# Gate vectors by one rounded product, bias and rounding on VectorE; queries split before they are turned; one weight pair loaded earlier

## The chip, the cores and the metric

The kernel runs on one core of a Trainium2 chip. The metric is device time in microseconds, from start to end of one launch: the median of three runs before the change is 1631.0 us (1630.05 to 1631.31).

## What is computed

One step of a two-layer network with width 1024 on 128 context tokens and 512 latent tokens (five token tiles of 128). Everything is float32. Each layer first makes six modulation vectors per group from a conditioning vector: shift, scale and gate of the mixer (c = 0, 1, 2) and of the MLP (c = 3, 4, 5).

```python
m = jax.nn.silu(cvec) @ w_mod + b_mod            # 1024 x 6144, per layer
hp = modulate(rmsnorm(xp, norm_mix_pre[layer]), mod_p[0], mod_p[1])
...
xp = xp + mod_p[2] * rmsnorm(yp, norm_mix_post[layer])      # gate c = 2
...
xp = xp + mod_p[5] * rmsnorm(sq_relu_mlp(hp, w_ffn_in[layer], w_ffn_out[layer]), norm_ffn_post[layer])
```

Layer 0's mixer is a gMLP beside an RG-LRU, layer 1's is attention with 16 query heads on 4 key heads of 64, window 128, a sink and 2-D rotary positions. Latent tokens also see cached context keys.

## The kernel before

A function `schedule()` writes one list of steps, and every engine walks that list in its order, waiting on semaphores. So the order of the list is the order of work on each engine. It also lists the weight loads; SP issues them in order into two slots of RAW (1 MB each), the next load waiting until its slot has been read.

**Products.** Float32 operands are split into a rounded part (float32r) and a remainder. Each product is three float32r matmuls (lines 1149 to 1151: high by high, low by high, high by low). For weights, ACT casts a block of RAW into the ring WH (line 630) and POOL subtracts to make WL (line 854); the ring has six blocks. Each step may carry a list "split" of blocks, which ACT and POOL handle behind the step's own work.

**Modulation.** A step `mod` multiplies the two columns of CL (conditioning vectors, padded to 32) with half a vector's weights: 16 plain float32 matmuls of 512 columns, in four groups of 32 PSUM rows. For a gate (c = 2 or 5) a seventeenth product of one row adds the bias from BMR into the open accumulation. VectorE copies the bank to PART. The next `mod`, or a `flush()`, first issues `modfin` for the former one. For a gate that is two plain float32 products with the selector SEL (one for context, one for latent tokens) that add the four row groups and spread them over 128 partitions; VectorE multiplies each into the gains GG (line 942). For other vectors it is four transposes (line 1210). Each layer has four gate halves, eight in all.

**MLP start.** `ffn()` issues the first weight pair's product for token tiles 0 and 1 (A, part 0), turns token tiles 3 and 4 (T, "cut"), runs the gate step (c = 5, half 0), then part 1 of the pair, then the second pair. The G2 steps are products with the second weights, one per token tile.

**Attention.** 20 units, of four heads by one token tile. Steps per unit i: S(i) scores; Q(i+1) turns the next queries; PV(i-2) transposes probabilities (line 1379) and multiplies with values (line 1387); sums; softmax(i) on VectorE (line 1114, mask and maximum) and ACT. Q turned each head's 128x64 block by a plain product with the identity (line 1340), twice, into both halves of the PSUM rows. ACT rounds the bank into QS (line 799), and VectorE subtracts the lower half from the bank (line 887, `query_remainder`), at the head of softmax.

Of the kernel before, what the change touches and what calls it, by code (L numbers as in the profile page):

```python
# [17 lines left out]
P = 128  # L18
# [18 lines left out]
def schedule():  # L37
# [23 lines left out]
    pend = []  # L61
# [8 lines left out]
    def mod(layer, c, half):  # L70
# [4 lines left out]
        pend.append((layer, c, half, cb[0]))  # L75
        cb[0] += 1
# [46 lines left out]
    def ffn(layer, fillers):  # L123
# [8 lines left out]
        ld = tiles(0, 0)  # L132
        T_(ph, TT - 2)
# [3 lines left out]
        tiles(2)  # L137
        for c in range(FC):
# [166 lines left out]
def hybrid_step(nc, A):  # L305
# [5 lines left out]
    with ctx:  # L311
# [26 lines left out]
        BMR = sb("BMR", [1, 512])  # L338
        IDN = sb("IDN", [P, P])
        SEL = sb("SEL", [P, 2, P])  # L340
# [25 lines left out]
        GGF = GG[:, :, :].rearrange("p v n -> p (v n)")  # L366
        RG = [GGF[:, i * TOK:(i + 1) * TOK] for i in range(6)]
# [10 lines left out]
        KTOK = GGF[:, 1024:2048].rearrange("p (s n) -> p s n", s=4)  # L378
        Z = GGF.rearrange("p (u h n) -> p u h n", u=2, h=4)

# [6 lines left out]
        PT = [RAW[:, PT_LOAD % RAWN, 512 * i:512 * i + 512] for i in range(4)]  # L387

# [22 lines left out]
        bmr_in = sem("bmr_in")  # L411
# [17 lines left out]
        k_out, k_hi, q_hi = sem("k_out"), sem("k_hi"), sem("q_hi")  # L429
# [170 lines left out]
        def _(act):  # L600
# [19 lines left out]
            act.dma_start(SEL[:, :, :], A["sel"]).then_inc(const_in[6], 16)  # L620
# [12 lines left out]
            for s in STEPS:  # L633
                k = s["kind"]
                if k == "mod":
                    if s["c"] in (2, 5):
                        if ngate:
                            upto(act, m_ready, GATE_M[ngate - 1])
                        ngate += 1
                        c0 = s["c"] * D + 512 * s["half"]  # L640
                        act.dma_start(BMR[:, :], A["b_mod"][s["layer"]:s["layer"] + 1, c0:c0 + 512]).then_inc(bmr_in, 16)

                        half, kind = s["half"], 0 if s["c"] == 2 else 2
                        if s["layer"] == 1:
                            for i in (18, 19):
                                upto(act, m_ready, PV_M[i])
                        elif kind:
                            act.wait_ge(x_new, TT)
                        else:
# [795 lines left out]
```

## Time and profile before

| | |
|---|---|
| median of three runs | 1631.0 us |
| the profiled execution's own time | 1628.96 us |
| its span | 1627.2 us |
| TensorE busy | 1506.1 us |
| VectorE / ACT / POOL busy | 656.2 / 554.5 / 518.1 us |
| mean granted TensorE clock | 0.968 of full speed |

The profile is one execution. The span runs from the first instruction to the last. TensorE's clock has two levels, 2.4 GHz (written 1.00) and 1.2 GHz (0.50). Rows of the timeline give start and duration in microseconds; matmuls are pipelined, so the distance between starts is their cost, and the written duration includes latency.

### The profile page before, as it was taken

What the parts mean: (1) busy time and instruction counts of PE and PEld (TensorE: products, weight loads), DVE (VectorE), ACT (ScalarE), POOL (GpSimd) and SP (SyncE); (2) the same over time, 40 slices, a digit from 0 to 9 for tenths busy, and PEclk for the clock granted to TensorE, in tenths of its full rate; (3) what the DMA queues carried; (4) which work ended last, traced back from release to release, by engine and by line L of the source; (5) the groups of instructions that cost most, each with busy time, mean ns of one, the idle gap of its engine ahead of it and who ended that gap; (6) DMA issues with size and microseconds to landing.
All of it is one profiled execution on the core that took longest, in us unless ns stands there. A gap on an engine that the chain in (4) does not pass through costs nothing.

```text
span 1627.2 us, 20069 instructions
## 1 busy us (share of the span) xinstructions
PE 1506.1 (93%) x8338; PEld 1242.4 (76%) x8338; DVE 656.2 (40%) x1124; ACT 554.5 (34%) x927; POOL 518.1 (32%) x224
## 2 busy tenths in 40 slices
PE   4799869899999999999889789989899999999997
PEld 1786646697898898998677656657689899989985
DVE  3665662733322322222644466623542232223225
ACT  3456732631221221232531266614532223222211
POOL 0521233141242243243234134413324234323330
PEclk9899979999999999999999899999899999999999
DMA  9322425144344342222022000033242122213201
GB/s 336 98 78 104 145 70 174 37 158 143 130 141 144 130 152 93 92 78 78 27 83 78 27 1 2 1 104 130 82 145 84 59 97 79 78 52 104 78 26 65
DMA packets 90498, 153.87 MB, mean 95 GB/s; under 512 B 6356, under 2 KB 44704, under 8 KB 90408
## 3 DMA queue, kind: packets, MB, share of 16 engines
q1 hardware_dynamic: 81712, 143.14, 26.7%
q10 hardware_dynamic: 8696, 9.45, 2.1%
q8 instruction: 66, 1.08, 0.3%
q14 instruction: 24, 0.20, 0.0%
HBM read 149.69 MB, written 2.89 MB: 94 GB/s over the span
## 4 chain that ended last, share of the span: by engine, by line
PE 71%; DVE 8%; ACT 5%; issue 2%; DMA 1%; POOL 1%; ACTq 0%; DVEq 0%; SPq 0%
PE PS L1149 20%; PE PS L1150 20%; PE PS L1151 20%; PE PS L1189 3%; PE PS L1387 2%; PE PS L1379 1%; DVE X L968 1%; DVE ACC L967 1%; PE PS L1357 1%; PE PS L1340 1%; PE PS L1358 1%; POOL WL L854 1%; ACT XCB L671 1%; DVE HL L988 1%; DVE HF L982 1%
## 5 line engine op out<-in xcount | busy, mean ns | idle before, releaser
L854 POOL TENSOR_TENSOR WL<-RAW,WH 128x1024 fp32r<-128x1024 f32 x172 | 422.0, 2484 | 769.2 <-ACT WH L630 769.2
L1149 PE MATMUL PS<-HH,WH 128*128 128x384 f32 (+1 forms) x1152 | 359.6, 312 | 10.4 <-DVE HL L988 5.3
L1151 PE MATMUL PS<-HH,WL 128*128 128x384 f32 (+1 forms) x1152 | 358.2, 311 | 0.0
L1150 PE MATMUL PS<-HL,WH 128*128 128x384 f32 (+1 forms) x1152 | 358.2, 311 | 0.0
L630 ACT CAST WH<-RAW 128x1024 fp32r<-128x1024 f32 x172 | 170.3, 1047 | 500.5 <-PE PS L1151 294.4
L1149 PE MATMUL PS<-WH,AH 128*128 128x512 f32 x640 | 253.3, 396 | 11.8 <-DVE AL L1003 6.5
L1150 PE MATMUL PS<-WL,AH 128*128 128x512 f32 x640 | 251.3, 393 | 0.0
L1151 PE MATMUL PS<-WH,AL 128*128 128x512 f32 x640 | 251.1, 392 | 0.0
L1149 PEld LDWEIGHTS PS<-HH,WH 128*128 128x128 f32 x1152 | 221.3, 192 | 16.1 <-issue 9.8
L1150 PEld LDWEIGHTS PS<-HL,WH 128*128 128x128 f32 x1152 | 221.5, 192 | 0.5
L1151 PEld LDWEIGHTS PS<-HH,WL 128*128 128x128 f32 x1152 | 220.9, 192 | 0.0
L1070 DVE TENSOR_TENSOR ACC<-ACC,PS 128x512 f32<-128x512 f32 x140 | 95.6, 687 | 233.3 <-PE PS L1151 233.3
L1001 DVE TENSOR_TENSOR XCB<-XCB 128x640 f32<-128x640 f32 x64 | 65.7, 1027 | 288.7 <-ACT XCB L718 288.5
L1149 PEld LDWEIGHTS PS<-WH,AH 128*128 128x128 f32 x640 | 121.1, 189 | 47.2 <-issue 8.6
L1149 PE MATMUL PS<-WH,HH 128*128 128x512 f32 x360 | 147.7, 410 | 8.7 <-POOL WL L854 5.4
L1150 PE MATMUL PS<-WL,HH 128*128 128x512 f32 x360 | 142.7, 396 | 0.0
L1151 PE MATMUL PS<-WH,HL 128*128 128x512 f32 x360 | 142.6, 396 | 0.0
L1151 PEld LDWEIGHTS PS<-WH,AL 128*128 128x128 f32 x640 | 121.3, 189 | 25.8
L1150 PEld LDWEIGHTS PS<-WL,AH 128*128 128x128 f32 x640 | 121.2, 189 | 24.7 <-issue 0.2
L718 ACT ACTIVATE XCB<-PS 128x640 f32<-128x640 f32 x64 | 45.1, 705 | 199.7 <-PE PS L1151 199.7
L1003 DVE TENSOR_TENSOR AL<-XCB,AH 128x640 fp32r<-128x640 f32 x64 | 76.7, 1198 | 50.7 <-ACT AH L724 50.7
L1149 PEld LDWEIGHTS PS<-WH,HH 128*128 128x128 f32 x360 | 69.1, 192 | 35.4 <-issue 10.9
(160 smaller groups left out, 1552.3 us busy)
## 6 DMA issues: line engine op xcount, KB each, us to landing
RAW<-in_w_mod SPq DMA_DIRECT2D x42, 1024.0 KB, 5.1
RAW<-in_w_ffn_in SPq DMA_DIRECT2D x32, 1024.0 KB, 5.7
RAW<-in_w_ffn_out SPq DMA_DIRECT2D x32, 1024.0 KB, 4.9
RAW<-in_w_in_even SPq DMA_DIRECT2D x8, 1024.0 KB, 6.8
RAW<-in_w_qkv SPq DMA_DIRECT2D x6, 1024.0 KB, 5.4
EARLY_H<-in_w_mod SPq DMA_DIRECT2D x4, 1024.0 KB, 21.2
RAW<-in_w_out_even SPq DMA_DIRECT2D x4, 1024.0 KB, 5.5
RAW<-in_w_out_odd SPq DMA_DIRECT2D x4, 1024.0 KB, 5.2
```

What stands on the lines that cost most here:

```text
L630: nc.scalar.copy(ring_view(WH, ld, j), w_view(ld, b)).then_inc(w_hi, 1)
L671: link(nc.scalar.activation(JUNK, ACC[:, t, :], ACT.Square, accum_out=STAT[:, t, 0:1]))
L718: nc.scalar.activation(XC[0], a_bank(a), ACT.Relu).then_inc(a_free[a % 2], 1)
L854: nc.gpsimd.tensor_tensor(ring_view(WL, ld, j), w_view(ld, b), ring_view(WH, ld, j).bitcast(f32), ALU.subtract).then_inc(w_lo, 1)
L1001: V_.tensor_tensor(XC[1], XC[0], XC[0], ALU.mult).then_inc(sq_ready, 1)
L1003: V_.tensor_tensor(AL[:, slot, :], XC[1], AH[:, slot, :].bitcast(f32), ALU.subtract).then_inc(a_lo, 1)
L1070: V_.tensor_tensor(acc, acc, bank, ALU.add).then_inc(b_free[b % 2], 1)
L1149: MM(out, wh, xh, start=first, stop=False)
L1150: MM(out, wh, xl, start=False, stop=False)
L1151: return MM(out, wl, xh, start=False, stop=last)
L1189: ins = MM(PS[32 * kt:32 * kt + 32, 6 + u % 2, :], CL[:, 4 * kh + kt, :], rv[:, kt, :], start=(kh == 0), stop=(kh == 1 and not gate))
L1387: ins = MM(PS[64 * par:64 * par + 64, 6 + u % 2, 0:256], vv(keys[kt])[:, HD * g:HD * g + HD], pt[:, par, :, :], start=(kt == 0), stop=(kt ...
```

## The change

Four edits:

1. CL gets its two columns a second time, so rows 2 and 3 of each group of 32 repeat rows 0 and 1. The bias product is gone. A new step `modsplit` on VectorE adds the bias to PART, rounds it into PARTR, and turns rows 2 and 3 into remainders with a per-partition factor (PICK). The selector SELR has ones for both, so `modfin` of a gate is one float32r product per token group. TensorE waits on `part_split` for it.
2. `modsplit` is put behind the next B group or the next G2 step.
3. Queries are split by VectorE on token rows (`query_split`: a cast and a subtraction, both from and to SBUF) before four transposes per unit; the ACT copy is the only later step, and `query_remainder` is gone.
4. In `ffn()` the load of the second pair stands ahead of the gate's two loads.

```diff
+    def modsplit():
+        if unsplit:
+            c, half = unsplit.pop()
+            step("modsplit", c=c, half=half)
     def flush():
+        modsplit()
         if pend:
...
     def bgroup(what, nb, t, j, ph=None):
         step("B", uses_b=1, frees=4 if t == TT - 1 else 0, what=what, nb=nb, t=t, j=j, ph=ph)
+        modsplit()
...
         ld = tiles(0, 0)
+        ld2 = load("acols", src=("w1", layer), col=2 * P)
         T_(ph, TT - 2)
         T_(ph, TT - 1)
         mod(*fill.pop(0))
         tiles(0, 1, ld)
-        tiles(2)
+        tiles(2, None, ld2)
...
                 step("G2", uses_b=2, frees=4 if t == TT - 1 else 0, layer=layer, c=c, t=t, j=j, ph=ph + 1)
+                modsplit()
                 if t in (0, 2) and fill and not last:
                     mod(*fill.pop(0))
...
-                    nc.scalar.copy(QS[:, i % 2, :], m_bank(u)).then_inc(q_hi, 1)
+                    nc.scalar.copy(QS[:, i % 2, :], m_bank(u)).then_inc(m_free[u % 2], 1)
...
+            def query_split(i):
+
+                g, t = i % NKV, i // NKV
+                if i > 1:
+                    upto(dve, m_ready, Q_M[i - 2])
+                q = ACC[:, t, 256 * g:256 * g + 256].rearrange("p (h d) -> p h d", h=4)
+                hi, lo = (Q2[i % 2].rearrange("p (h w d) -> p h w d", h=4, w=2)[:, :, w, :] for w in (0, 1))
+                V_.tensor_copy(hi.bitcast(f32r), q).then_inc(q_hi, 1)
                 dve.wait_ge(q_hi, i + 1)
-                V_.tensor_tensor(QS[64:128, i % 2, :], m_bank(u)[64:128, :], QS[64:128, i % 2, :].bitcast(f32),
-                                 ALU.subtract).then_inc(m_free[u % 2], 1)
+                V_.tensor_tensor(lo, q, hi, ALU.subtract).then_inc(q_split, 1)
...
+                elif k == "modsplit":
+                    ngate += 1
+                    upto(dve, m_free, part_u)
+                    dve.wait_ge(bmr_in, 16 * ngate)
+                    V_.tensor_tensor(PART[0:4, :], PART[0:4, :], bias_row(s["c"], s["half"]), ALU.add).then_inc(bias_read, 1)
+                    dve.wait_ge(bias_read, ngate)
+                    if ngate == 1:
+                        dve.wait_ge(sel_made, 1)
+                    link(V_.tensor_copy(PARTR[:, :], PART[:, :]))
+                    V_.scalar_tensor_tensor(PARTR[:, :], PARTR[:, :].bitcast(f32), PICK[:, 2:3], PART[:, :], ALU.mult, ALU.add)\
+                        .then_inc(part_split, 1)
...
-                                MM(PS[0:32, 6 + u % 2, :], SEL[0:1, 0, 0:32], BMR[:, :], start=False, stop=True)
...
                     if s["c"] in (2, 5):
+                        ngate += 1
+                        pe.wait_ge(part_split, ngate)
                         for v in (0, 1):
                             u = s["m"] + v
                             m_acquire(u)
-                            MM(m_bank(u), SEL[:, v, :], PART[:, :], start=True, stop=True).then_inc(m_ready[u % 2], 1)
+                            MM(m_bank(u), SELR[:, v, :], PARTR[:, :], start=True, stop=True).then_inc(m_ready[u % 2], 1)
...
-                    for h in range(4):
-                        c = HD * (4 * g + h)
-                        for half in (0, 64):
-                            ins = MM(m_bank(u)[half:half + 64, P * h:P * h + P], ACC[:, t, c:c + HD], IDN[:, :], start=True, stop=True)
+                    pe.wait_ge(q_split, s["n"] + 1)
+                    for h in range(4):
+                        ins = TR(m_bank(u)[:, P * h:P * h + P], Q2[s["n"] % 2][:, P * h:P * h + P], IDN[:, :])
```

**VectorE at the first gate half of layer 0's MLP.** COPY ACC is the first token tile of the first G2 steps, GG the gains. Before:

```order
L1001 TENSOR_TENSOR XCB<-XCB 128x640 [waits a_lo,a_hi,a_free1]
L1003 TENSOR_TENSOR AL<-XCB,AH 128x640 [waits a_hi]
L1072 COPY ACC<-PS 128x512 [waits b_ready0]
L1072 COPY ACC<-PS 128x512 [waits b_ready1]
L942 TENSOR_TENSOR GG<-PS,GG 128x512 [waits gg_in0,m_ready0]
L942 TENSOR_TENSOR GG<-PS,GG 128x512 [waits gg_in0,m_ready1]
L932 COPY PART<-PS 128x512 [waits m_ready1,m_ready0]
```

The same place in the changed kernel:

```order
L1047 TENSOR_TENSOR XCB<-XCB 128x640 [waits a_lo,a_hi,a_free1]
L1049 TENSOR_TENSOR AL<-XCB,AH 128x640 [waits a_hi]
L1120 COPY ACC<-PS 128x512 [waits b_ready0]
L1120 COPY ACC<-PS 128x512 [waits b_ready1]
L972 TENSOR_TENSOR PART<-PART,GG 4x512 [waits bmr_in,m_free1]
L976 CAST PARTR<-PART 128x512 [waits bias_read]
L977 SCALAR_TENSOR_TENSOR PARTR<-PARTR,PICK,PART 128x512 [waits dve_done]
L988 TENSOR_TENSOR GG<-PS,GG 128x512 [waits gg_in0,m_ready0]
L988 TENSOR_TENSOR GG<-PS,GG 128x512 [waits gg_in0,m_ready1]
L966 COPY PART<-PS 128x512 [waits m_ready1,m_ready0]
```

Three operations now stand between the copies of the G2 step and the product that TensorE issues right behind that step. The `modfin` follows at once in the list here, and likewise in layer 1.

**VectorE in a late attention unit.** AST holds the softmax's small values, COPY RAW moves turned probabilities. Before:

```order
L1120 SCALAR_TENSOR_TENSOR AST<-AST,SINK 128x4 [waits z_ready]
L1121 TENSOR_SCALAR AST<-AST 128x4 [waits dve_done]
L1122 TENSOR_TENSOR AST<-SINK,AST 128x4 [waits dve_done]
L895 TENSOR_TENSOR HL<-PS,HH 128x2x128 [waits mix_hi]
L504 COPY RAW<-PS 128x512 [waits m_ready1,pt_mm0]
L504 COPY RAW<-PS 128x512 [waits m_ready1,pt_mm1]
L1130 TENSOR_TENSOR AST<-AST 128x4 [waits es_ready,e_ready]
L1131 RECIPROCAL AST<-AST 128x4 [waits dve_done]
L887 TENSOR_TENSOR QS<-PS,QS 64x512 [waits q_hi]
L1114 ISA GG,AST<-PS,XCB 128x512 [waits s_done,pt_mm1]
```

And in the changed kernel:

```order
L1166 SCALAR_TENSOR_TENSOR AST<-AST,SINK 128x4 [waits z_ready]
L1167 TENSOR_SCALAR AST<-AST 128x4 [waits dve_done]
L1168 TENSOR_TENSOR AST<-SINK,AST 128x4 [waits dve_done]
L920 TENSOR_TENSOR HL<-PS,HH 128x2x128 [waits mix_hi]
L911 CAST PART<-ACC 128x4x64 [waits m_ready0]
L913 TENSOR_TENSOR PART<-ACC,PART 128x4x64 [waits q_hi]
L523 COPY RAW<-PS 128x512 [waits m_ready1,pt_mm0]
L523 COPY RAW<-PS 128x512 [waits m_ready1,pt_mm1]
L1176 TENSOR_TENSOR AST<-AST 128x4 [waits es_ready,e_ready]
L1177 RECIPROCAL AST<-AST 128x4 [waits dve_done]
L1160 ISA GG,AST<-PS,XCB 128x512 [waits s_done,pt_mm1]
```

The one subtraction ahead of the mask step has become two operations that stand earlier, behind the former unit's softmax.

**POOL around layer 0's MLP start.** WL rows are weight remainders, HL rows the remainders of turned token tiles. Before:

```order
L835 TENSOR_TENSOR GG<-GG 128x640 [waits a_free1,h_ready]
L837 TENSOR_TENSOR MX<-MX,GG 128x640 [waits h_sum]
L854 TENSOR_TENSOR WL<-RAW,WH 128x1024 [waits w_hi] x10
L849 TENSOR_TENSOR HL<-HF,HH 128x4x128 [waits h_hi] x5
L854 TENSOR_TENSOR WL<-RAW,WH 128x1024 [waits w_hi] x64
```

And POOL at this place in the changed kernel:

```order
L855 TENSOR_TENSOR GG<-GG 128x640 [waits a_free1,h_ready]
L857 TENSOR_TENSOR MX<-MX,GG 128x640 [waits h_sum]
L874 TENSOR_TENSOR WL<-RAW,WH 128x1024 [waits w_hi] x10
L869 TENSOR_TENSOR HL<-HF,HH 128x4x128 [waits h_hi] x2
L874 TENSOR_TENSOR WL<-RAW,WH 128x1024 [waits w_hi] x2
L869 TENSOR_TENSOR HL<-HF,HH 128x4x128 [waits h_hi] x3
L874 TENSOR_TENSOR WL<-RAW,WH 128x1024 [waits w_hi] x62
```

Two weight blocks (the second pair) moved between the token tiles' remainders 1 and 2; ACT's two casts for them moved with them, ahead of the norm of token tile 4.

## Rows read from the trace of the kernel before

**Rows 1.** The page: busy times, and the chain that ended last.

```profile
PE 1506.1 (93%) x8338; PEld 1242.4 (76%) x8338; DVE 656.2 (40%) x1124; ACT 554.5 (34%) x927; POOL 518.1 (32%) x224
...
PE 71%; DVE 8%; ACT 5%; issue 2%; DMA 1%; POOL 1%; ACTq 0%; DVEq 0%; SPq 0%
```

**Rows 2.** Timeline of TensorE (start, duration): gate steps in layer 0's MLP.

```profile
371.20 1.88 PE L1205 MATMUL PS<-PART,SEL 128*128 128x512 f32 x4
373.01 1.90 PE L1189 MATMUL PS<-RAW,CL 128*32 128x512 f32 x10
...
376.80 0.50 PE L1149 MATMUL PS<-WH,AH 128*128 128x512 f32 x1
```

**Rows 3.** The same timeline: the following modulation step, which is no gate.

```profile
389.63 1.92 PE L1189 MATMUL PS<-RAW,CL 128*32 128x512 f32 x16
391.48 0.50 PE L1149 MATMUL PS<-WH,AH 128*128 128x512 f32 x1
```

**Rows 4.** The same timeline: the kernel's first step, and the gate step at MLP start.

```profile
9.18 3.64 PE L1189 MATMUL PS<-RAW,CL 128*32 128x512 f32 x16 [9.18 <-DVE CL L873]
...
321.10 2.59 PE L1189 MATMUL PS<-RAW,CL 128*32 128x512 f32 x10 [1.98 <-DVE HF L982]
...
327.48 0.69 PE L1149 MATMUL PS<-HH,WH 128*128 128x384 f32 x1
```

**Rows 5.** Timeline of VectorE beside Rows 2.

```profile
371.40 0.69 DVE L1072 COPY ACC<-PS 128x512 f32<-128x512 f32 x1 [1.70 <-PE PS L1151]
372.25 0.69 DVE L942 TENSOR_TENSOR GG<-PS,GG 128x512 f32<-128x512 f32 x1 [0.17 <-PE PS L1205]
```

**Rows 6.** The page's costliest groups (busy, mean ns | idle); durations of L988 (min/median/max).

```profile
L854 POOL TENSOR_TENSOR WL<-RAW,WH 128x1024 fp32r<-128x1024 f32 x172 | 422.0, 2484 | 769.2 <-ACT WH L630 769.2
...
L988 DVE TENSOR_TENSOR HL<-HF,HH x20: 691/1224/2886, 40.6 to 1161.6; 128x512 fp32r<-128x512 f32 x20
```

**Rows 7.** Windows: busy time of PE, PEld, DVE, ACT, POOL; granted clock; DMA.

```profile
769.70:775.90 6.20, 5.82 (x14) 4.56 (x15) 0.62 (x2) 1.36 (x2) 4.70 (x2) 0.50 0.01 4
1144.50:1147.20 2.70, 0.07 (x2) 0.04 (x1) 2.68 (x3) 2.05 (x5) 1.64 (x1) 1.00 0.00 0
1148.00:1151.20 3.20, 3.20 (x19) 3.20 (x18) 3.13 (x7) 3.17 (x9) 0.00 (x0) 0.53 0.00 0
```

**Rows 8.** Timeline around layer 0's MLP start.

```profile
308.10 0.57 ACT L759 COPY ACC<-PS 128x512 f32<-128x512 f32 x1
...
317.98 1.15 PE L1221 MATMUL PS<-IDN,ACC 128*128 128x128 f32 x8 [1.19 <-DVE HF L982]
...
323.42 1.26 POOL L849 TENSOR_TENSOR HL<-HF,HH 128x512 fp32r<-128x512 f32 x1 [2.64 <-ACT HH L702]
...
329.61 2.00 ACT L630 CAST WH<-RAW 128x1024 fp32r<-128x1024 f32 x2 [6.28 <-DMA RAW<-in_w_ffn_in]
```

**Rows 9.** Timeline of late attention units.

```profile
981.15 1.09 PE L1340 MATMUL PS<-IDN,ACC 128*64 128x128 f32 x16
...
989.34 1.09 PE L1340 MATMUL PS<-IDN,ACC 128*64 128x128 f32 x16
...
994.25 0.69 DVE L1114 CUSTOM_DVE_ANT_0 GG<-PS,XCB 128x512 f32<-128x512 f32 x1 [0.79 <-PE PS L1379]
...
997.30 0.42 DVE L895 TENSOR_TENSOR HL<-PS,HH 128x256 fp32r<-128x256 f32 x1
...
998.02 1.09 PE L1340 MATMUL PS<-IDN,ACC 128*64 128x128 f32 x16
...
999.04 1.09 PE L1379 MATMUL PS<-IDN,GG 128*128 128x128 f32 x8
```

**Rows 10.** Timeline of the first attention units.

```profile
915.44 2.55 DVE L1052 TENSOR_TENSOR ACC<-ACC,GG 128x512 f32<-128x512 f32 x1
...
918.02 0.70 DVE L887 TENSOR_TENSOR QS<-PS,QS 64x512 fp32r<-64x512 f32 x1
...
926.18 1.98 PE L1340 MATMUL PS<-IDN,ACC 128*64 128x128 f32 x16
```

More of the change, by code:

```diff
@@ L75, in mod @@
         pend.append((layer, c, half, cb[0]))
+        if c in (2, 5):
+            unsplit.append((c, half))
         cb[0] += 1
@@ L337, in hybrid_step @@
         PART = sb("PART", [P, 512])
-        BMR = sb("BMR", [1, 512])
+        Q2B = alias("Q2B", [P, 512])
+        PARTR = sb("PARTR", [P, 512], f32r)
         IDN = sb("IDN", [P, P])
-        SEL = sb("SEL", [P, 2, P])
+        SELR = sb("SELR", [P, 2, P], f32r)
+        PICK = sb("PICK", [P, 3])
         CC = sb("CC", [P, 2, KD])
@@ L387, in hybrid_step, with bias_row @@
         PT = [RAW[:, PT_LOAD % RAWN, 512 * i:512 * i + 512] for i in range(4)]
+        def bias_row(c, half):
+            return GG[0:4, 3 if c == 2 else 0, 512 * half:512 * half + 512]
         def vv(t):
@@ L636, in _ @@
                     if s["c"] in (2, 5):
+                        half, kind = s["half"], 0 if s["c"] == 2 else 2
+                        if kind:
+                            act.wait_ge(x_new, TT if s["layer"] == 0 else 3 * TT)
+                        elif s["layer"] == 1:
+                            for i in (18, 19):
+                                upto(act, m_ready, PV_M[i])
+                        else:
+                            act.wait_ge(rg_done, 4)
+                            act.wait_ge(sel_made, 1)
                         if ngate:
-                            upto(act, m_ready, GATE_M[ngate - 1])
+                            act.wait_ge(bias_read, ngate)
                         ngate += 1
                         c0 = s["c"] * D + 512 * s["half"]
[L641 to L649, printed above, removed]
-                            act.wait_ge(rg_done, 4)
+                        act.dma_start(bias_row(s["c"], half), A["b_mod"][s["layer"]:s["layer"] + 1, c0:c0 + 512].broadcast_to([4, 512]))\
+                            .then_inc(bmr_in, 16)
                         g = A["norm_mix_post" if kind == 0 else "norm_ffn_post"][s["layer"]:s["layer"] + 1, 512 * half:512 * half + 512]
@@ L907, in _ @@
                 elif k == "lambda":
+                    dve.wait_ge(const_in[5], 16)
+                    dve.wait_ge(const_in[6], 16)
+                    low = IDN[:, :].rearrange("p (g w) -> p w g", g=4)[:, 2:4, :]
+                    link(V_.tensor_reduce(PICK[:, 0:2], low, AX.X, ALU.add))
+                    for v in (0, 1):
+                        V_.tensor_scalar(SELR[:, v, :], SELF[:, v, :], PICK[:, v:v + 1], None, ALU.add)
+                    link(V_.tensor_tensor(PICK[:, 2:3], PICK[:, 0:1], PICK[:, 1:2], ALU.add))
+                    V_.tensor_scalar(PICK[:, 2:3], PICK[:, 2:3], -1.0, None, ALU.mult).then_inc(sel_made, 1)
                     lam = PC[:, LAM:LAM + 8]
@@ L1180, in _ @@
                     if s["n"] == 0:
-                        pe.wait_ge(cl_ready, 1)
+                        pe.wait_ge(cl_ready, 2)
                     for kh in (0, 1):
```

35 lines of the change are left out of this document (14 added, 21 removed).

## The prediction

> **What bounds the kernel now.** I read the page first: TensorE is busy 93% of the span, and 71% of the chain that ended last is its work [rows 1]. So I take the kernel as a queue of matmuls. An edit is worth what it takes from TensorE's queue or adds to it as waiting; work on other engines counts where TensorE waits for it. I then read TensorE's timeline at the gate steps, VectorE's beside it, the granted clock behind long waits, and the attention units, where TensorE and VectorE release each other in turn.
>
> **The gate steps without the bias product.** In the timeline a gate step runs from 373.01 to 376.80, 3.79 us [rows 2]. A step with the same sixteen products and no bias takes 389.63 to 391.48, 1.85 us [rows 3]. The difference, 1.94 us, is more than the bias product itself, since the four row groups no longer overlap around it. Six of the eight gate halves run at the full clock: 6 x 1.94 = 11.6 us less. The other two open an MLP; they are worked out below with the moved load.
>
> **The two selector products.** For a gate they take 371.20 to 373.01, 1.81 us for two products [rows 2]. The trace has float32r products of 512 columns everywhere; one lasts 0.50 us [rows 3], half of it latency that overlaps with the next, so I take 0.25 us each, 0.5 for both. What follows decides how much of the 1.3 us counts:
>
> - Three gate halves are followed by a token tile's product, which needs neither bank: 3 x 1.3, say 3.8 us less.
> - Three are followed by the next modulation step with no wait for rounding. That step needs the first bank back from VectorE. VectorE first finishes the token tile's copy (from 0.20 us after the products' start, for 0.69) and then multiplies 0.69 [rows 5], so the bank is free at about 0.2 + 0.69 + 0.03 + 0.69 = 1.6 us where it was 1.8. That is 0.2 us less each, 0.6 in all.
> - Two, one per layer (the first half of c = 5), get the new wait.
>
> **The new wait.** There `modsplit` stands directly ahead of `modfin`: both come behind the same G2 step, so the rounding isn't hidden by a group at all. VectorE's queue after the last matmul, from 0: wait and copy until 0.89 [rows 5]; bias add over 512 columns, a subtraction of that width takes 0.69 when undisturbed [rows 6], until 1.61; the cast, which no row shows, between half of that and all of it (0.35 and 0.69; I take 0.5, since a single input should cost less), until 2.15; the multiply-add, of the same width, 0.7, until 2.9; a hand-over of 0.05 to 0.1. TensorE stands from 0.2 to 3.0. Its first product takes 0.45 with latency, VectorE's multiply 0.17 + 0.69 [rows 5], so the next modulation step starts at 4.4 instead of 1.81. That is 2.6 us later, twice: +5.2 us. With the cast's bounds it is 2.4 to 2.8 each.
>
> The clock adds to it. After TensorE had stood for some 2.6 us at 1144.5 to 1147.2, the granted clock was 0.53 from 1148.0 to 1151.2; another wait, ahead of 769.7, was followed by 6.2 us at 0.50 [rows 7]. Half speed costs half of that, 1.5 and 3.1 us. The new wait (2.8 us, then 0.8 more before the modulation step) is as long. I take 2.0 each, +4.0 us, with bounds 0 and 6.2.
>
> **The MLP start and the moved load.** The gate step there began at the low clock and, with its bias, lasted 321.10 to 327.48, 6.4 us; sixteen products without bias at the low clock take 3.64 [rows 4], 2.7 less. But ACT now casts the pair's two blocks behind the copy at 308.10, 2.00 us [rows 8], ahead of the norm of token tile 4. That tile was turned at 317.98, when a wait for VectorE ended, a few tenths after it was ready; its norm now comes 2.0 us later, and POOL, with two weight blocks of 2.5 us each [rows 6], may slow VectorE beside it. I count the turn and the gate step 1.3 to 2.2 us later. POOL's last remainder, at 323.42 + 1.26 [rows 8], moves too, to about 326 to 327, and part 1 of the pair needs it: so it starts 0.5 to 1.4 us earlier than 327.48. In layer 1 the same. Together -1.9 us. The second half of the gate's load now waits until POOL has both blocks; with the casts done near 310.7 and the blocks at 2.5 us each that is near 315. The old pair's load could start only when the first half of the step at 321.10 was read, and was there at 329.61 [rows 4, 8], so a load takes at most 7 us or so: the gate's second half is there near 321 to 322, and is read a microsecond into a step that starts at 322.4. What is no longer needed is the wait for this pair behind the step.
>
> **Queries.** On TensorE, Q took 998.02 to 999.04, 1.02 us [rows 9]; eight transposes of whole 128 columns take as long as the sixteen halves did (1.09 and 1.09), so four cost 0.6 with the hand-over: -0.4 us per unit if TensorE alone counts. But VectorE must now split before it. In a late unit: the mask step starts at 994.25, when the last transposes are done, and the remainder of a former unit ends at 997.72 [rows 9]. Then come cast and subtraction of 256 columns. L895, of that size, takes 0.42, so 0.33 to 0.42 and 0.42, with hand-overs 0.85 to 0.95: the queries are ready at 998.6, 0.6 us after TensorE wanted them. The late start eats the shorter step: 998.6 + 0.6 is 999.2 against 999.04. The subtraction taken out (L887) doesn't help, since the mask step waited for TensorE anyway. Where the unit was shorter, as 981.15 to 989.34 (8.19 us against 8.68 [rows 9]), the VectorE chain is the longer by about 0.6. Of the twelve late units, four lose 0.2, two 0.1 and six about 0.5: +4.0 us.
>
> In the first six units it is the other way. There TensorE waits for VectorE and ACT, and L887 (0.70) lies on the path; a unit at the low clock turns its queries in 1.98 us [rows 10], which halves. I take -1.9 for each of two units and -0.7 for each of four: -6.6 us. Against it, the first split waits behind VectorE's last rotary addition, which ended at 917.99, where only L887 had to follow [rows 10]; now follow two splits, four transposes and a copy, 1.4 us more undisturbed. Beside POOL an addition of that width, 0.69 us undisturbed [rows 6], took 2.55 [rows 10], and POOL's weight blocks still run then: up to 2.6. I take 2.0. Attention in sum: 4.0 - 6.6 + 2.0 = -0.6 us, bounds -5 and +4.
>
> The Trainium skill says of this contention ("GPSIMD Engine Reference", Specifications) that POOL shares its SBUF interface with VectorE instructions that have two SBUF inputs or a two-port mode. The old subtraction had one SBUF input, the new one has two. By that rule alone the first unit would be at the 2.6 end; the row of 2.55 us agrees with it.
>
> **The rest** hides: six small VectorE operations for SELR and PICK stand where VectorE waits for ACT before the convolution, the second copy of CL is 0.2 us in front of a first product whose successor waits for its load, and rounding at the six other gate halves has a whole product group of over 5 us before its reader.
>
> **Sum.** -11.6 - 3.8 - 0.6 + 5.2 + 4.0 - 1.9 - 0.6 = -9.3 us. The profiled execution took 1628.96 us by its own time, the span and 1.8 us around it; it would become 1619.7. It lies 2.0 below the median of the runs, so the median goes from 1631.0 to 1621.7 us.
>
> **Rivals.**
>
> - *The new waits keep the clock up* (the two G2 waits too short, or masked by the products between): the 4.0 us fall away, and with the early attention units at their best (-5) it is 1613. For it: 1144.5 to 1147.2 itself ran at 1.00, only what came behind was slow [rows 7]. Chance 0.20.
> - *No difference.* VectorE's splits run beside POOL in the late units also, or the low clock stays as long behind each new wait as in its longest row, and the moved load gives nothing: +3 to +4 in attention, +2.2 for the clock, +1.9: 1629 to 1630. Chance 0.10.
> - *Slower: TensorE's clock falls in attention.* Every unit loses 0.86 us of plain products and gets transposes, and TensorE waits 0.6 us before them. If the granted clock then stays at 0.50 for further units, each pays: Q took 1.98 against 1.09 [rows 9, 10], and a late unit of 8.7 us, most of it TensorE, would take some 5 us more. Two such units cancel the gain, three give 1636. Against it: late units, with twelve or sixteen transposes each, ran at the full pace already [rows 9]. Chance 0.08. The Trainium skill has a rule that speaks for it ("TensorE: Matmul & The Clock Gate", Part 4: PE-mode transpose): in its words the full clock "doesn't engage" for transposes. By that rule this rival is what happens, and the time is its 1636 or more; no row here decides it.
>
> The forecast itself, 1617 to 1626, has the remaining 0.62.
>
> **Numbers.** A measurement of this kernel tells 0.2% (3.3 us) from no change. Faster needs under 1627.7: all of 0.62 and 0.20, and a little of the second rival: 0.83. Within 0.2%: 0.10. Slower: 0.07. The range 1612 to 1629 takes in the bounds of the clock (0 to 6.2), of attention and of the cast.
>
> **What would show it.** Gate steps of 1.85 us at six places and no row of BMR. A wait of TensorE of 2.5 to 3 us for VectorE's rounding (L977) once per layer at the start of the G2 steps, then a stretch at clock 0.50. In late units, TensorE waiting 0.5 us for L913 before the transposes, with unit lengths near 8.8 us; in the first ones shorter units. Part 1 of the first weight pair 0.5 to 1.4 us earlier than the sum to that point has it. It is wrong if the two G2 waits are absent, if the gate's second load is waited for, or if the clock of attention falls.

## The result, and the profile after

The changed kernel takes 1639.2 us (median of 6 runs, 1634.7 to 1644.4) against 1630.5 (6 runs) for the kernel before: ratio 1.0055, 95% interval 1.0041 to 1.0069. It is slower, where 9.3 us less was forecast. A second set of runs gave 1638.4 against 1630.7, 1.0048 (1.0036 to 1.0061). Its profiled execution took 1634.66 us with a span of 1632.9, 5.7 us over that of before.

The page of the changed kernel, in answer to [rows 1]:

```profile
PE 1472.6 (90%) x8066; PEld 1232.1 (75%) x8066; DVE 685.6 (42%) x1174; ACT 553.8 (34%) x927; POOL 521.2 (32%) x224
...
PE 65%; DVE 13%; ACT 5%; issue 2%; DMA 1%; POOL 1%; ACTq 0%; DVEq 0%
```

TensorE is busy for 33.5 us less and its part of the chain falls from 71% to 65%; VectorE's rises from 8% to 13%. Work left TensorE, and more of the time now goes into waits for VectorE.

To find the places I matched the two timelines by a product that both kernels run 2152 times in the same order (the line of the high-by-high products, L1149 before, L1195 after), and read how much later or earlier each starts than in the trace of before. The table gives the change of that distance over each stretch. A trace is one execution; the second column of the same program shows how far two differ.

| Stretch (start in the trace of before) | Forecast | Changed kernel | The same, second trace | Best version (`three`, below) |
|---|---|---|---|---|
| Front, to 208.6 us | 0 | +9.0 | +8.8 | -0.4 |
| Layer 0, c = 2 gates, to 309.8 | -5.4 | -3.2 | -3.2 | -4.1 |
| Layer 0, MLP start, to 341.5 | -1.0 | +2.0 | +4.1 | +0.8 |
| Layer 0, c = 5 gates, to 402.5 | +2.5 | +0.1 | +1.3 | -2.5 |
| MLP, QKV and attention, to 1074.6 | -0.6 | -1.3 | -1.3 | -3.4 |
| Layer 1, c = 2 gates, to 1148.0 | -5.4 | -4.0 | -4.1 | -4.5 |
| Layer 1, MLP start, to 1176.7 | -1.0 | +0.9 | +1.4 | +0.3 |
| Layer 1, first c = 5 gates, to 1524.7 | +2.7 | +3.5 | +3.7 | +4.2 |
| Last gate half | -1.3 | -1.3 | -1.3 | -1.3 |

**The front.** Nothing was forecast there, and it is more than the whole loss: 9.0 us in a trace that is 5.7 us longer in all. First VectorE, then POOL, ACT, ACT's DMA issues and TensorE of the changed kernel (start, duration):

```profile
61.36 0.16 DVE L937 TENSOR_REDUCE PICK<-IDN 128x2 f32<-128x8 f32 x1
61.56 3.46 DVE L939 TENSOR_SCALAR SELR<-GG,PICK 128x128 fp32r<-128x128 f32 x2
64.94 2.35 DVE L940 TENSOR_TENSOR PICK<-PICK 128x1 f32<-128x1 f32 x1
67.33 0.15 DVE L941 TENSOR_SCALAR PICK<-PICK 128x1 f32<-128x1 f32 x1
67.40 2.26 DVE L945 TENSOR_SCALAR LG<-PC 128x8 f32<-128x8 f32 x1
69.69 2.32 DVE L946 TENSOR_TENSOR LG<-PC,LG 128x8 f32<-128x8 f32 x1
...
62.55 9.44 POOL L874 TENSOR_TENSOR WL<-RAW,WH 128x1024 fp32r<-128x1024 f32 x4
...
72.04 0.21 ACT L677 ACTIVATE LG<-LG 128x8 f32<-128x8 f32 x1 [5.72 <-DVE LG L946]
72.05 2.69 ACTq L683 DMA_DIRECT2D MX<-in_rg_wa  x4
74.76 2.64 ACTq L683 DMA_DIRECT2D MX<-in_rg_wi  x4
77.44 0.69 ACT L732 COPY MX<-PS 128x640 f32<-128x640 f32 x1 [5.19 <-issue]
...
78.39 0.55 PE L1195 MATMUL PS<-HH,WH 128*128 128x256 f32 x1 [5.52 <-ACT MX L732]
```

Read upwards, this is a chain. TensorE waits 5.52 us for ACT's copy of a PSUM bank; ACT has eight DMA issues to do before the copy, and ahead of those an Exp (L677) that waits 5.72 us for VectorE's L946. Ahead of L946 stand the selector operations (L937 to L941), 6.0 us long. In the trace of before, the same Exp and the same copy:

```profile
62.21 2.31 DVE L912 TENSOR_TENSOR LG<-PC,LG 128x8 f32<-128x8 f32 x1
...
65.89 0.21 ACT L657 ACTIVATE LG<-LG 128x8 f32<-128x8 f32 x1
...
69.98 0.70 ACT L712 COPY MX<-PS 128x640 f32<-128x640 f32 x1 [3.88 <-issue]
```

The stall costs more than its length, since TensorE then runs at half speed for five microseconds (window of the changed kernel: from and to, length, busy time of PE, PEld, DVE, ACT and POOL, granted clock, DMA share and GB/s):

```profile
78.40:83.40 5.00, 5.00 (x23) 5.00 (x24) 0.00 (x0) 2.22 (x3) 3.65 (x2) 0.50 0.23 62
```

**The gate steps** are as forecast on TensorE: the modulation step takes 266.87 to 268.72, 1.85 us. But at the second half of c = 2 the rounding is late even where a product group lies ahead of its reader. Changed kernel, VectorE, POOL and TensorE:

```profile
275.10 2.45 DVE L972 TENSOR_TENSOR PART<-PART,GG 4x512 f32<-4x512 f32 x1
277.59 2.52 DVE L976 CAST PARTR<-PART 128x512 fp32r<-128x512 f32 x1
280.14 0.75 DVE L977 SCALAR_TENSOR_TENSOR PARTR<-PARTR,PICK,PART 128x512 fp32r<-128x512 f32 x1
...
274.61 5.21 POOL L874 TENSOR_TENSOR WL<-RAW,WH 128x1024 fp32r<-128x1024 f32 x2 [38.05 <-ACT WH L649]
...
280.99 0.70 PE L1246 MATMUL PS<-PARTR,SELR 128*128 128x512 f32 x2 [1.10 <-issue]
281.53 0.40 PE L1195 MATMUL PS<-WH,HH 128*128 128x512 f32 x1
```

Three operations that take 0.67, 0.43 and 0.75 us undisturbed (next rows) take 5.7 here. TensorE waits 1.10 and then spends 0.54 on the products, 1.64 in all, where the old step took 1.31 (it began at 273.46 before): the 0.8 us gain is a 0.3 us loss.

At the second half of c = 5 in layer 1 the same happens, and there the rounding holds up something else, VectorE's copies of the token tile behind it (VectorE, POOL and TensorE of the changed kernel):

```profile
1227.43 2.40 DVE L972 TENSOR_TENSOR PART<-PART,GG 4x512 f32<-4x512 f32 x1
1229.87 2.51 DVE L976 CAST PARTR<-PART 128x512 fp32r<-128x512 f32 x1
...
1226.89 5.21 POOL L874 TENSOR_TENSOR WL<-RAW,WH 128x1024 fp32r<-128x1024 f32 x2 [24.25 <-ACT WH L649]
...
1233.83 0.50 PE L1195 MATMUL PS<-WH,AH 128*128 128x512 f32 x1 [1.60 <-DVE ACC L1120]
```

TensorE waits 1.60 us for a bank that VectorE hasn't copied yet; the kernel before has no wait there. So three of the eight roundings (both second halves of c = 2 and this one) meet POOL's blocks, in every trace of this document.

**The new wait** at (5,0), the first half of c = 5, VectorE and then TensorE of the changed kernel:

```profile
379.77 0.67 DVE L972 TENSOR_TENSOR PART<-PART,GG 4x512 f32<-4x512 f32 x1
380.47 0.43 DVE L976 CAST PARTR<-PART 128x512 fp32r<-128x512 f32 x1
380.93 0.75 DVE L977 SCALAR_TENSOR_TENSOR PARTR<-PARTR,PICK,PART 128x512 fp32r<-128x512 f32 x1
...
381.79 0.70 PE L1246 MATMUL PS<-PARTR,SELR 128*128 128x512 f32 x2 [2.67 <-issue]
383.04 1.92 PE L1233 MATMUL PS<-RAW,CL 128*32 128x512 f32 x16 [0.55 <-DVE GG L988]
```

**The MLP start**, ACT, VectorE, POOL, TensorE, and the load on SP's queue, in answer to [rows 4, 8]:

```profile
314.88 1.99 ACT L649 CAST WH<-RAW 128x1024 fp32r<-128x1024 f32 x2
316.77 1.06 ACT L691 ACTIVATE XCB<-ACC 128x1024 f32<-128x1024 f32 x1
...
318.48 3.35 DVE L1013 SCALAR_TENSOR_TENSOR ACC<-ACC,STAT,GG 128x1024 f32<-128x1024 f32 x1
321.86 2.19 DVE L1014 TENSOR_TENSOR X<-X,ACC 128x1024 f32<-128x1024 f32 x1
...
316.00 4.74 POOL L874 TENSOR_TENSOR WL<-RAW,WH 128x1024 fp32r<-128x1024 f32 x2 [1.88 <-ACT WH L649]
320.74 2.23 POOL L869 TENSOR_TENSOR HL<-HF,HH 128x512 fp32r<-128x512 f32 x1
...
327.97 1.94 PE L1262 MATMUL PS<-IDN,ACC 128*128 128x128 f32 x8 [4.86 <-DVE HF L1028]
330.66 1.08 PE L1233 MATMUL PS<-RAW,CL 128*32 128x512 f32 x4 [0.75 <-DVE HF L1028]
...
320.77 0.37 SPq L608 DMA_DIRECT2D RAW<-in_w_mod  x1
```

The casts push the norm of token tile 4 back by 1.8 us (2.0 forecast: L691 starts 2.4 us behind the copy at 314.41, and 0.6 behind it without casts). POOL's second block now runs beside the first of VectorE's two operations of 1024 columns, and the token tile's remainder (L869), late behind the blocks, beside the other. They took 1.28 and 1.23 us undisturbed, and take 3.35 and 2.19 here. So the wait of 1.19 us in [rows 8] is 4.86. The next one, 1.98 us in [rows 4], is 0.75. Part 1 of the pair starts at 334.39, 6.9 us later than before, where the product ahead of the turns (314.73) was 6.3 later: 0.6 us later, where 0.5 to 1.4 us earlier was forecast.

### The profile page after: what moved, and what is told of

It is laid out like the page before. It is cut to its first block, busy times and chain, and to the rows that moved or that the text cites. A ratio compares the mean times of both kernels' runs of the same rounds, so it can differ in the third digit from the quotient of the medians.

```text
span 1632.9 us, 19600 instructions
## 1 busy us (share of the span) xinstructions
PE 1472.6 (90%) x8066; PEld 1232.1 (75%) x8066; DVE 685.6 (42%) x1174; ACT 553.8 (34%) x927; POOL 521.2 (32%) x224
## 4 chain that ended last, share of the span: by engine, by line
PE 65%; DVE 13%; ACT 5%; issue 2%; DMA 1%; POOL 1%; ACTq 0%; DVEq 0%
PE PS L1195 20%; PE PS L1197 19%; PE PS L1196 19%; DVE GG L1160 2%; PE PS L1233 2%; DVE ACC L1013 2%; DVE X L1014 2%; PE PS L1415 1%; PE PS L1423 1%; DMA RAW<-in_w_ffn_in 1%; ACT XCB L691 1%; ACT WH L649 1%; POOL WL L874 1%; DVE HF L1028 1%; ACT XCB L701 1%
## 5 line engine op out<-in xcount | busy, mean ns | idle before, releaser
L1195 PE MATMUL PS<-HH,WH 128*128 128x384 f32 (+1 forms) x1152 | 361.2, 314 | 19.1 <-ACT MX L732 5.5
L1195 PE MATMUL PS<-WH,AH 128*128 128x512 f32 x640 | 253.1, 395 | 13.4 <-DVE AL L1049 6.5
L1195 PEld LDWEIGHTS PS<-HH,WH 128*128 128x128 f32 x1152 | 222.4, 193 | 24.9 <-issue 18.6
L1195 PEld LDWEIGHTS PS<-WH,AH 128*128 128x128 f32 x640 | 121.2, 189 | 49.3 <-issue 8.7
L1195 PE MATMUL PS<-WH,HH 128*128 128x512 f32 x360 | 146.9, 408 | 6.3 <-POOL WL L874 3.0
L1195 PEld LDWEIGHTS PS<-WH,HH 128*128 128x128 f32 x360 | 69.0, 192 | 32.0 <-issue 10.7
```

Source lines behind the costliest of these rows:

```text
L1195: MM(out, wh, xh, start=first, stop=False)
```

## The experiments

The kernels were timed in four sets, each beside the kernel before (medians 1630.0, 1630.7, 1629.6 and 1630.4 us). Each is the changed kernel with the edit shown. The changed kernel itself stands in the second set alone, so a difference of medians between two sets is also a difference of sets; the ratios are free of that.

| Kernel | Selector block | Rounding of (5,0) | Second pair | Queries | Median us | Ratio, 95% interval |
|---|---|---|---|---|---|---|
| changed | first | late | early load | split first | 1638.4 | 1.0048 (1.0036 to 1.0061) |
| `sel_late` | last | late | early load | split first | 1629.8 | 0.9998 (0.9989 to 1.0007) |
| `sel_wait` | in the wait | late | early load | split first | 1629.3 | 0.9993 (0.9984 to 1.0002) |
| `load_old` | first | late | as before | split first | 1638.0 | 1.0048 (1.0036 to 1.0060) |
| `split_early` | first | early | early load | split first | 1630.9 | 1.0010 (1.0000 to 1.0020) |
| `q_old` | first | late | early load | as before | 1637.7 | 1.0048 (1.0035 to 1.0061) |
| `sel_split` | last | early | early load | split first | 1623.5 | 0.9955 (0.9942 to 0.9969) |
| `mid` | last | early | early load | split first | 1623.9 | 0.9957 (0.9945 to 0.9969) |
| `three` | last | early | as before | split first | 1620.8 | 0.9938 (0.9926 to 0.9950) |
| `four` | last | early | as before | as before | 1623.2 | 0.9948 (0.9931 to 0.9964) |
| `cast_late` | last | early | early load, late casts | split first | 1636.4 | 1.0043 (1.0031 to 1.0055) |
| `cast_q` | last | early | early load, late casts | as before | 1634.7 | 1.0032 (1.0020 to 1.0043) |

### The selector block (`sel_late`, `sel_wait`)

```diff
                 elif k == "lambda":
...
-                    link(V_.tensor_reduce(PICK[:, 0:2], low, AX.X, ALU.add))
...
-                    V_.tensor_scalar(PICK[:, 2:3], PICK[:, 2:3], -1.0, None, ALU.mult).then_inc(sel_made, 1)
                     lam = PC[:, LAM:LAM + 8]
...
                     V_.tensor_scalar(NCL[:, :], acc, -0.5, None, ALU.mult).then_inc(lam_ready, 1)
...
+                    link(V_.tensor_reduce(PICK[:, 0:2], low, AX.X, ALU.add))
...
+                    V_.tensor_scalar(PICK[:, 2:3], PICK[:, 2:3], -1.0, None, ALU.mult).then_inc(sel_made, 1)
```

> The changed kernel, with the selector and PICK operations moved behind the last operation of the lambda step. Theory A: their slow run beside POOL's weight blocks holds the lambda step up by about 6 us, ACT waits for it before it copies the first bank, TensorE stands 5.5 us and then runs at the low clock; nearly all of the 9 to 10 us that are lost before 170 us come back, so about 1629 us against 1639 for the changed kernel, and no TensorE wait for the first copy. Rival: the stage is late for another reason (the first product's start, the clock's phase), and the time stays within 2 us of 1639.

Measured: 1629.8 us, 8.6 less than the changed kernel (8.2 by the ratios) and level with the kernel before: theory A. In its trace (ACT) the Exp and the copy are back in their places, and TensorE doesn't wait for the copy:

```profile
65.65 0.21 ACT L677 ACTIVATE LG<-LG 128x8 f32<-128x8 f32 x1
...
69.92 0.70 ACT L732 COPY MX<-PS 128x640 f32<-128x640 f32 x1 [4.06 <-issue]
```

The second kernel puts the block two operations later only, behind the one with `lam_e` and ahead of `dve.wait_ge(lam_e, 2)`.

> The changed kernel with the selector block two instructions later: behind the two lambda operations that ACT's Exp waits for, ahead of VectorE's own wait for that Exp. This is the place that the prediction spoke of. Theory A (only the order against those two operations counts, the block's 6 us beside POOL's weight blocks are free once ACT has its input): ACT's Exp near 66 us, its first copy of MX near 70, no wait of TensorE for it, 1629 to 1631 us as with the block at the step's end. Rival (the block delays NCL, the convolution or POOL from there also): 2 us or more above that, with TensorE waiting 2 us or more longer than before at the first products that need the convolution.

Measured: 1629.3 us, theory A again. Here the block takes 7.3 us (6.0 in the changed kernel), and costs nothing (VectorE of `sel_wait`):

```profile
63.25 2.30 DVE L937 TENSOR_TENSOR LG<-PC,LG 128x8 f32<-128x8 f32 x1
...
65.67 4.61 DVE L943 TENSOR_SCALAR SELR<-GG,PICK 128x128 fp32r<-128x128 f32 x2
70.20 2.37 DVE L944 TENSOR_TENSOR PICK<-PICK 128x1 f32<-128x1 f32 x1
```

So it is neither the operations nor their slowness alone, but their standing ahead of the two that ACT waits for.

### The rounding at (5,0) (`split_early`, `sel_split`)

```diff
         T_(ph, TT - 1)
         mod(*fill.pop(0))
+        modsplit()
         tiles(0, 1, ld)
```

> The changed kernel, with the bias and rounding of the first half of c = 5 placed right behind its gate step instead of behind the first G2 step. Theory C: the two waits of 2.7 us are due to that place alone; TensorE then waits only for VectorE's multiply, 0.9 us at most, so 2.3 us less in each layer plus what the low clock cost in layer 1 (about 1.5): 1632 to 1634. Rival: the rounding now runs beside POOL's blocks, takes over 5 us and holds up VectorE's squares: no gain, 1638 or more.

Measured: 1630.9 us, 7.5 to 8.3 under the two medians of the changed kernel, more than theory C gave. Alone it could not be told from the front's loss, so both edits were joined:

> Two edits of the changed kernel at once: the selector block behind the last lambda operation, and the rounding of (5,0) directly behind its product. Theory A (the two losses lie at different places and add up: 9.4 us at the front, 6 to 8 at the two (5,0) steps): 1622 to 1624 us, that is 6 to 8 under the kernel before, and no wait over 1 us for either. Rival (part of both is the same thing, low clock that falls at other places when a wait goes): 1626 to 1629.

Measured: 1623.5 us, 6.3 under `sel_late`: the losses add up, theory A. `sel_split` is also the first version that beats the kernel before. In each of the traces with this edit, the stretch of layer 0's c = 5 gates comes 2.4 to 2.5 us ahead of before; without it it is 0.1 to 2.8 us behind. The rounding isn't slow in its new place (0.68, 0.43 and 0.75 us at 336.0 in the trace of `split_early`), and TensorE waits 0.93 us for VectorE's multiply (1218.0), as theory C has it.

In layer 1 the same edit gives less. The first c = 5 gates there are 3.5 to 5.1 us behind before without it, and still 1.5 to 4.2 with it. Most of what is left is the wait behind the second half: 0.3 to 1.9 us in the traces without the edit, 1.8 to 2.1 in all seven with it, and there each time a stretch at clock 0.50 follows. Wait and clock together cost 3.7 to 4.0 us with the edit and 0.6 to 2.2 without. No experiment took this rounding away from POOL's blocks, so what it would give is open.

The spread in layer 0 fits the clock. The changed kernel's (5,0) wait was 2.67 us in one trace and 2.66 in the other, and what followed was not the same (windows of the first and of the second trace, at the products behind the modulation step):

```profile
384.90:388.10 3.20, 3.20 (x18) 2.62 (x15) 0.80 (x2) 0.00 (x0) 0.00 (x0) 1.00 0.83 280
```

```profile
384.50:388.00 3.50, 3.14 (x17) 0.60 (x16) 1.16 (x2) 0.00 (x0) 0.00 (x0) 0.59 0.65 126
```

### The second pair's load (`load_old`, `three`, `mid`, `cast_late`)

`load_old` puts the load back behind the gate's two loads (`tiles(2)` without `ld2`).

> The changed kernel, with the second weight pair's load back behind the gate's loads. Theory B: the pair's casts and POOL blocks ahead of token tile 4's norm cost 3.7 us at each MLP start (4.9 us waits of TensorE for the turned tile, each followed by the low clock) and more in layer 1; taking them back gives 6 to 8 us, about 1632. Rival: the shorter gate step uncovers the old load, TensorE waits 2 to 3 us for the pair's remainder at each start, and half or more of the gain is gone: 1636 or above.

Measured: 1638.0 us, ratio 1.0048, equal to the changed kernel and in the rival's range. The wait of 4.9 us is gone, and one of 3.9 us (ACT's activation of the pair's first product, behind casts that waited for the DMA) has come at 344.54. With the other two faults mended:

> The two edits of sel_split, and the second pair's load behind the gate's again, as in the kernel before. Theory B (the moved load costs, since the two casts delay the norm of token tile 4 and VectorE's work beside POOL: 5 us of waiting at either MLP start, of which the old order gets 1 to 2 us each back after its own wait for the pair): 2 to 4 us less than sel_split. Rival 1 (what undoing it alone gave, 1.3 us, is all): 0 to 1.5 less. Rival 2 (the moved load gives something once the rest is undisturbed, as forecast): 1 to 2 more.

Measured: 1620.8 us, 2.7 under `sel_split`, where theory B has it. But the intervals of the two ratios overlap; taken together they leave some 3 us either way, so rival 1 isn't excluded. Over all traces but the two with late casts, the stretch of layer 0's MLP start costs 2.9 us against before with the early load (mean of 8 traces) and 3.0 with the old one (mean of 3): the wait only changes its name. In layer 1 it is +1.6 against -1.0; only there does the old order win. `three` at that product in layer 0 (TensorE):

```profile
333.94 0.35 PE L1194 MATMUL PS<-HH,WH 128*128 128x256 f32 x1 [3.00 <-ACT XCB L738]
```

> The two edits of sel_split, and the second pair's load between the last two transposes of the MLP start and the gate's loads: ahead of the gate loads still, but its casts behind the norm of token tile 5. Theory B: the wait of 4.9 us before token tile 4 goes, the wait for the pair's first block of the old order (3.9 us) does not come or is under 2 us, since the load is still early: 3 to 6 us less than sel_split and below three. Rival: the casts then keep ACT from the copies behind token tile 5 and the wait only moves: within 1.5 us of sel_split.

Measured: 1623.9 us (0.9957), but nothing on the theory: loads are numbered by their order among loads alone, no load lies between the two places, and the instructions came out as in `sel_split`. It is a second measurement of that kernel, 0.5 us from the first.

To hold back the casts, not the load:

```diff
         T_(ph, TT - 1)
+        loads[ld2]["hold"] = len(steps)
         mod(*fill.pop(0))
...
-        at = max([at, i] + [mod_step[ld] for ld in range(max(0, owner[j] - 9), owner[j] - 1) if ld in mod_step])
+        at = max([at, i, loads[owner[j]].get("hold", 0)] + [mod_step[ld] for ld in range(max(0, owner[j] - 9), owner[j] - 1) if ld in mod_step])
```

> The two edits of sel_split with the second pair's load still ahead of the gate's, but ACT's two casts of it (and so POOL's two weight blocks) held back until the gate's modulation step, behind the norms of token tiles 4 and 5. Theory B (not the early load but the early casts cost: they delay the norm, and POOL's blocks stretch VectorE's two operations of 1024 columns from 2.5 to 5.5 us): the wait of 4.9 us before the last two transposes falls to 1 to 2 us as in the kernel before, the old order's wait of 3.9 us for the pair does not come, and the time is 1616 to 1620 us, below three (1620.8). Rival: casts and blocks meet the rounding of the gate vectors and the first products' copies instead: 1620 to 1624.

Measured: 1636.4 us, a clear miss of both theories. The first half of theory B holds (the waits are 1.19 us before the last turned tile and 1.98 before the gate step, as in the kernel before), but the gate step is torn in two. TensorE, POOL and SP's queue of `cast_late`:

```profile
318.79 1.93 PE L1234 MATMUL PS<-RAW,CL 128*32 128x512 f32 x8 [1.98 <-DVE HF L1029]
332.56 1.94 PE L1234 MATMUL PS<-RAW,CL 128*32 128x512 f32 x8 [11.83 <-DMA RAW<-in_w_mod]
...
322.45 4.64 POOL L876 TENSOR_TENSOR WL<-RAW,WH 128x1024 fp32r<-128x1024 f32 x2
...
327.12 0.37 SPq L610 DMA_DIRECT2D RAW<-in_w_mod  x1
```

RAW has two places. The pair sits in one of them until POOL has read it, and only at 327.12, right behind POOL's last block, can the gate's second half be asked for. So here a load that stands ahead of the gate's must be cast early, whatever that costs the norm. Against `sel_split` the late casts cost 13 us, in two places: the two MLP starts are 9.9 and 9.1 us behind before, where its trace has 4.1 and 0.6.

### The queries (`q_old`, `four`, `cast_q`)

Each takes `query_split` out and puts the old sixteen half transposes and `query_remainder` back.

> The changed kernel, with the queries turned by plain products and split as before. Theory D: early units gain about 5 us from the new form and late ones lose about 4, so the old form is 0 to 2 us slower in the attention stage: 1639 to 1641. Rival: the splits on VectorE cost more than they give in this stage, and the old form is 2 us or more faster: below 1637.

> cast_late with the queries of the kernel before. Theory (the split queries give what the trace shows, 1 us in attention): 1 us over cast_late, within 0.5. Rival (their undoing alone gave 0.8 to 1.6 us, so they cost that): 0.8 to 1.6 under cast_late.

> three with the queries of the kernel before: what is left of the change is the rounded gate vectors alone, without the stall at the front and without the wait at (5,0). By the terms that the trace of the changed kernel bears out (bias products 6 x 1.9, selector products 6 x 1.2 with what follows them) 10 to 13 us under the kernel before: 1618 to 1621. Rival (some of it is given back as low clock or as waits elsewhere): 1621 to 1625. Against three the theories on the queries are as in cast_q: 1 us over it, or 0.8 to 1.6 under.

Measured: 1637.7, 1634.7 and 1623.2 us. Against its twin, the old way is 0.8 us faster, 1.7 faster and 2.4 slower. The signs differ and each is within the two intervals: the queries' effect is below what these runs tell, some 2 us either way. Neither theory is decided. `four` is the change's gate vectors alone, with the two faults mended. It is 6.4 us under the kernel before (ratio 0.9948), where the terms gave 10 to 13: the rival, though its fastest run (1616.1) is beyond both. Its trace shows two of the places where the rest went: 4.6 us more at layer 0's MLP start, and a wait of 1.86 us behind layer 1's second c = 5 rounding, beside POOL.

> The changed kernel once more, beside the kernel before and the three next ones, so that they have a level on one chip. Expected 1638 to 1640 us, 0.5% to 0.6% over the kernel before, if its 1639.2 was the kernel's own. Rival: six runs spread over 1634.7 to 1644.4 had a high median by chance, then 1635 to 1637, and the queries and the moved load, whose undoing gave 1637.7 and 1638.0, cost or gave nothing; the rounding taken ahead (1630.9) would then be worth 4 to 6 us and not 8.

It gave 1638.4 us, the level that the expectation gives first; the rival's is 1635 to 1637.

## Why the prediction was wrong

**The step that failed** is "The rest hides: six small VectorE operations for SELR and PICK stand where VectorE waits for ACT before the convolution". VectorE does wait for ACT there, but for the Exp whose input the two next operations make, and the block was put ahead of these two. The 1.6 us of waiting were behind these two, and none in front. Undoing this alone gives 8.6 us, and moving it behind them, ahead of the wait that I had meant, gives as much. The trace of before had the warning: an operation of 128x8 elements took 2.31 us there (62.21, L912), beside POOL's blocks. I costed neither that nor the order.

This step is not the whole miss. Without it the kernel takes 1629.8 us, level with the kernel before (0.9998) and still 8 us over the forecast. In the stretches of its trace (`sel_late`) the two MLP starts are 7.8 us worse than forecast, the c = 5 gates 2.7 and the c = 2 gates 2.1; the attention stretch is 0.9 better.

**The second half of that step**, that rounding "has a whole product group of over 5 us before its reader", failed as well: beside POOL the three operations take 5.7 us, and TensorE waited 1.10 us at 280.99, 1.01 at 1115.36 and 1.60 at 1233.83, the last for copies that stand behind the rounding. The first two are why the steps of the c = 2 gates gave 4.0 us in either layer and not 5.4. (The table has 3.2 for layer 0: 1.6 us are lost ahead of the steps, between 208 and 238 us, in the changed kernel's two traces and not in that of `sel_late`.) The wait of 1.16 us at 266.27 is no part of it: the kernel before waits 0.54 us there (257.59), and that step is 0.4 us shorter, for 0.2 forecast.

**The MLP start and the moved load** were mis-sized and had the wrong sign: +2.9 us (+5.5 in the second trace) for -1.9. I had the 2.0 us of the casts and named POOL, but gave its contention 0.2 us at most; it cost 3.0 at VectorE's two wide operations (3.35 + 2.19 against 1.28 + 1.23). That alone is larger than the gain of the shorter gate step there (2.7).

**What held.** The plain gate step is 1.85 us. The three rounding operations took 0.67, 0.43 and 0.75 for 0.72, 0.5 and 0.7; the wait is 2.67 us and 0.55 more for the first bank. For the clock behind (5,0) 2.0 us each were forecast, with bounds 0 and 3.1. Of the twelve such waits in the six traces that have them, one was followed by clock 1.00 alone, seven by a low stretch that cost 1.7 us and four by one of 3.1 to 3.4; the changed kernel's two traces lost 1.7 and 3.4 in the two places together. The last gate half is at -1.3 as forecast. The rounding ahead gave 6.3 to 8 us where wait and clock were priced at 9.2; the wait behind the second half in layer 1 took some of it.

**Attention.** The stretch with it is 1.3 us shorter for a forecast of 0.6, and late units show the wait that was forecast (0.44 us for the split, for 0.6; TensorE and VectorE of the changed kernel). But they take 8.57 us, where [rows 9] have 8.68 and 8.8 was expected:

```profile
1005.33 0.63 PE L1376 MATMUL PS<-IDN,Q2B 128*128 128x128 f32 x4 [0.44 <-DVE Q2B L913]
...
1004.43 0.29 DVE L911 CAST Q2B<-ACC 128x256 fp32r<-128x256 f32 x1
1004.75 0.42 DVE L913 TENSOR_TENSOR Q2B<-ACC,Q2B 128x256 f32<-128x256 f32 x1
```

With the old queries that stretch is 0.4 to 2.5 us shorter than before in three traces, and with the new ones 1.0 to 3.4 in ten, so the agreement proves nothing for the term. Its three parts can be read from the starts of the units' scores, counted from the last product ahead of attention. The first scores come 3.9 us later in all ten traces with the new queries, where 2.0 was forecast, at most 2.6. Two of the 3.9 are the cast of the first split, which is held beside POOL (VectorE and POOL of the changed kernel; a cast of that size takes 0.29 us at 1004.43).

```profile
925.66 2.24 DVE L911 CAST PART<-ACC 128x256 fp32r<-128x256 f32 x1
...
922.66 5.09 POOL L874 TENSOR_TENSOR WL<-RAW,WH 128x1024 fp32r<-128x1024 f32 x2 [19.98 <-ACT WH L649]
```

The first six units then gain 6.7 us in five of these traces, the changed kernel's two among them, for 6.6 forecast. That it fits is luck in part: the clock was at 0.50 for 3 us of them there, and for 13.7 in the trace of before. In the five others, with 11 to 18 us at 0.50, they gain 4.3 to 4.8. The later units lose 1.0 to 1.9 us for a forecast of 4.0. So two parts were mis-sized, by 1.9 and by over 2 us, and cancel. The prediction looked to the new subtraction, with its two SBUF inputs; it ran in 0.43 us behind POOL's block (927.94), and what was held is the cast, with one.

The slower rival (the clock falls in attention) didn't happen. Four late units of the changed kernel, the granted clock being the third number from the end:

```profile
996.80:1031.00 34.20, 30.72 (x208) 20.80 (x209) 22.11 (x72) 20.08 (x53) 14.40 (x4) 1.00 0.00 1
```

With twenty transposes of whole columns in each (four of queries, sixteen of probabilities) among 32 other matmuls, the units ran at 1.00. The Trainium skill's rule ("TensorE: Matmul & The Clock Gate", Part 4) that the full clock "doesn't engage" for transposes doesn't describe units in which matmuls stand between them; this row decides against it here. The slower outcome came from a place that no rival named.

## What to carry to other kernels

A few tiny operations on an engine that isn't the bottleneck are free only behind the last thing that another engine waits for. Before calling them hidden, find the next hand-over on their own engine and see on which side of it they stand; here the same block costs 9 us or nothing. Beside POOL's long operations, count VectorE's operations by number and not by size: in these traces one that is held took some 2 to 3 us, with 1 column or 512. And look at what else stands behind them in the queue, not only at their own reader. And a load that is moved ahead brings its casts, its weight blocks and its buffer's next user with it: in layer 0 the wait at one place only became a wait at another.

## What the runs showed of the hardware

In the selector block, a VectorE operation beside POOL's weight blocks ended when a block ended, whatever its size. In the first fence of the front, POOL's four blocks run from 62.55 for 9.44 us, which makes them end near 64.9, 67.3, 69.6 and 72.0 if they are even; VectorE's operations end at 65.02, 67.29, 69.66 and 72.01, with 128x128, 128x1, 128x8 and 128x8 elements. A 4x512 addition took 2.45 us for 0.67, a 128x512 cast 2.52 for 0.43. Where an operation has more to do it runs on: the 128x1024 one of 3.35 us at 318.48 ended at 321.83, 1.1 us behind the block. Not every operation is held: 0.15 us at 67.33, right behind the end of a block, and 0.16 us at 61.36, ahead of the first; and four that read PSUM (L1028 at 315.45, the last two within the block of 316.00) took 1.36 us together, as at 308.98 without POOL. The Trainium skill ("GPSIMD Engine Reference", Specifications) has sharing for operations with two SBUF inputs or a two-port mode. These rows agree as to the two-input ones, L940, L946 and L972. L945 and the casts L976 and L911 have one SBUF input and were held too; whether they run in such a mode no run here shows.

One wait of the same 2.7 us in two executions of one program left the clock at 1.00 once and at 0.59 in the window shown once. Over six traces of five programs, twelve such waits cost 0 once, 1.7 us seven times and 3.1 to 3.4 us four times in low clock. Of a wait of that length in this kernel, the clock's part can't be had from one trace.
